# Slab slots, an earlier cache output and a product on GpSimd, in a streaming encoder layer on eight cores

## The reference: what is computed

```
h = rms_norm(x, pre_mix_w); p = h @ w_in      # 1024 x 3584: q k v g | B C hc, 512 columns each
q, k = rotary(q), rotary(k) * 128**-0.5       # 4 heads of 128
o, S = retention in chunks of 64, with decay  # a carried 128 x 128 state per head
o = rms_norm per head(o) * ret_norm_w * silu(g)
y = B * causal_dwconv3(C * hc)
x = x + rms_norm(concat[o, y] @ w_out, post_mix_w)
h2 = rms_norm(x, pre_ffn_w)
u = causal_dwconv3(h2 @ w_up)                 # 1024 x 4096
f = (gelu(u) * (h2 @ w_gate)) @ w_down        # 4096 x 1024
x = x + rms_norm(f, post_ffn_w)
```

## Time and profile before

| what | value |
|---|---|
| median of 3 runs | 2011.95 us (2008.78 to 2012.05) |
| the profiled execution | 2010.04 us |
| its span, core 4, the slowest | 2008.5 us; the other cores 1995.5 to 2005.7 us |
| TensorE busy | 1957.7 us |
| VectorE, ScalarE, GpSimd busy | 1273.2, 970.8, 492.0 us |
| moved by DMA | 369.12 MB, 184 GB/s on average |

### The profile page before, as it was taken

One profiled execution on the slowest core, in us unless ns is written; L12 is line 12 of the kernel. 1 busy time (PEld: TensorE's weight loads), 2 busy tenths in 40 slices (PEclk: granted clock), 3 DMA queues, 4 the chain that ended last, 5 costly groups with the idle time before them and its releaser, 6 DMA issues.

```text
span 2008.5 us, 29808 instructions; the slowest of 8 cores (1995.5 to 2008.5 us)
## 1 busy us (share of the span) xinstructions
PE 1957.7 (97%) x10823; PEld 936.3 (47%) x10823; DVE 1273.2 (63%) x2317; ACT 970.8 (48%) x1922; POOL 492.0 (24%) x1031
## 2 busy tenths in 40 slices
PE   6998999999999999999999999999999999999998
PEld 3453444454444444444444444444444444444443
DVE  6777856667668655674656836668356664567456
ACT  6576685763444453344533445434434445334423
POOL 3653211101422421123221332114121242212001
PEclk9999999999999999999999999999999999999999
DMA  9945888977446634464434643446343553435433
GB/s 283 268 145 163 263 279 273 307 248 258 143 158 204 225 132 157 157 203 147 159 138 178 220 152 116 166 151 230 140 152 130 184 215 126 168 120 190 156 126 117
DMA packets 109955, 369.12 MB, mean 184 GB/s; under 512 B 8952, under 2 KB 43856, under 8 KB 97648
## 3 DMA queue, kind: packets, MB, share of 16 engines
q1 hardware_dynamic: 109536, 367.11, 53.7%
q10 hardware_dynamic: 272, 0.10, 0.0%
HBM read 313.50 MB, written 53.68 MB: 183 GB/s over the span
## 4 chain that ended last, share of the span: by engine, by line
PE 89%; DMA 5%; DVE 2%; ACT 2%; issue 1%; POOL 0%; ACTq 0%; POOLq 0%; SPq 0%; DVEq 0%
PE pF L933 37%; PE pF L1022 20%; PE pM L743 10%; PE pM L782 7%; PE pM L881 5%; DMA x_sb<-xp 2%; PE pM L933 2%; PE pF L743 2%; PE pM L1022 1%; DMA v_sb<-w_down 1%; PE pT L644 1%; PE pT L687 1%; PE pF L782 1%; PE pF L881 1%; DMA kte<-w_gate 1%
## 5 line engine op out<-in xcount | busy, mean ns | idle before, releaser
L933 PE MATMUL pF<-hT,wug 128*128 128x512 bf16 x3856 | 867.2, 380 | 8.8 <-DMA wug<-wug_s 2.1
L933 PEld LDWEIGHTS pF<-hT,wug 128*128 128x128 bf16 x3856 | 373.6, 98 | 448.9 <-issue 5.9
L1022 PE MATMUL pF<-wdn,act 128*128 128x512 bf16 x1846 | 423.9, 380 | 6.0 <-DVE act L944 2.8
L936 ACT ACTIVATE up_sb<-pF 128x512 f32<-128x512 f32 x241 | 143.2, 594 | 344.2 <-PE pF L933 341.6
L939 DVE SCALAR_TENSOR_TENSOR acc<-up_sb,cvec,acc 128x512 f32<-128x512 f32 x256 | 192.4, 752 | 158.7 <-ACT acc L938 158.1
L1022 PEld LDWEIGHTS pF<-wdn,act 128*128 128x128 bf16 x1846 | 179.5, 98 | 219.1 <-DVE act L944 4.1
L944 DVE TENSOR_TENSOR act<-pF,gl 128x512 bf16<-128x512 f32 x230 | 158.4, 689 | 143.3 <-ACT gl L943 127.7
L937 POOL COPY halo_f<-up_sb 128x2 f32<-128x2 f32 x256 | 61.1, 239 | 641.8 <-ACT up_sb L936 641.1
L943 ACT ACTIVATE gl<-acc 128x512 bf16<-128x512 f32 x256 | 160.0, 625 | 118.8 <-DVE acc L941 118.3
L743 PE MATMUL pM<-slab,hT 128*128 128x512 bf16 x856 | 202.6, 383 | 3.8 <-ACT slab L591 2.9
L941 DVE SCALAR_TENSOR_TENSOR acc<-up_sb,cvec,acc 128x512 f32<-128x512 f32 x256 | 198.9, 778 | 5.0
(11 more groups left out here) (380 smaller groups left out, 2242.7 us busy)
## 6 DMA issues: line engine op xcount, KB each, us to landing
wug<-wug_s SPq DMA_DIRECT2D x208, 512.0 KB, 3.8
wdn<-wdn_s SPq DMA_DIRECT2D x28, 2048.0 KB, 8.0
slab<-slab_s SPq DMA_DIRECT2D x54, 1024.0 KB, 5.1
x_sb<-xp SPq DMA_DIRECT2D x32, 512.0 KB, 6.4
stg<-w_up SPq DMA_DIRECT2D x32, 512.0 KB, 9.0
wug_s<-wug SPq DMA_DIRECT2D x32, 512.0 KB, 9.3
yp<-x_sb SPq DMA_DIRECT2D x31, 512.0 KB, 4.2
stg<-w_in SPq DMA_DIRECT2D x18, 512.0 KB, 9.9
```

Of the source, the lines that this page charges most:

```text
L933: op("pe", [lambda e, k=k, u=u, pp=pp: e.matmul(pp[:, :nt], lhsT=wug[:, sl, u, k, :], rhs=hT[:, k, :nt], start=(k == 0), stop=(k == 7)) fo ...
L936: op("act", lambda e: e.activation(out=upv[:, 2:2 + nt], in_=PU[:, :nt], func=AF.Copy), [RU, RUP], [RUP], c_act(nt))
L1022: op("pe", [lambda e, q=q, hs=hs, m=m, cols=cols, pd=pd: e.matmul(pd[:m, :], lhsT=al[q][0][:, cols], rhs=wdn[:, cs_[q] % 8, hs], start=(q ...
```

## The change

It has three parts. In the first mixers there is a fourth slab slot, over wug 2 and 3, and a fixed table says which slab goes where (`SLOT_1`, by slab number: slab 2 to slot 3, 0 to 1, 1 to 2, 3 to 0, 6 to 1, 5 to 3, 4 to 2, 7 to 0, 8 to 1); the staging buffers there are three from the start. The caches of the 16 tokens are put out at the end of the second ffn stage instead of the end of the program. The product with the weight vector at the end of an ffn row group runs on GpSimd, with a planner cost of 2.55 us, except where the row group is ended in halves. `UG_0` and `SL_LEAD` only name values that stood there already.

```diff
+GW_POOL = True
+SLOT_1 = (1, 2, 3, 0, 2, 3, 1, 0, 1)
+UG_0 = 2
+SL_LEAD = 12.0
...
-    STG_M = STG + [(wug[:, q].rearrange("p u k j -> p (u k j)").bitcast(F32), [("wug", q, u, kc) for u in range(2) for kc in range(8)]) for q in range(2, NWUG)]
+    STG_M = STG
...
-    slab_x = wug[:, 0:2].rearrange("p a u k j -> p (a u k j)").rearrange("p (k c) -> p k c", c=512)
-    SLABX = [[("wug", k // 4, (k % 4) // 2, 4 * (k % 2) + q) for q in range(4)] for k in range(8)]
+    slab_x = [wug[:, b:b + 2].rearrange("p a u k j -> p (a u k j)").rearrange("p (k c) -> p k c", c=512) for b in (0, 2)]
+    SLABX = [[[("wug", b + k // 4, (k % 4) // 2, 4 * (k % 2) + q) for q in range(4)] for k in range(8)] for b in (0, 2)]
     def load_slab(first, g):
-        sl = nxt("slab", 3 if first else 2)
-        dst, kk_ = (slab_x, SLABX) if sl == 2 else (SLABS[sl][0], [[k] for k in SLABS[sl][1]])
+        sl = SLOT_1[g] if first else nxt("slab", 2)
+        dst, kk_ = (slab_x[sl - 2], SLABX[sl - 2]) if sl > 1 else (SLABS[sl][0], [[k] for k in SLABS[sl][1]])
-                if g == 8:
-                    ring[0] = STG
-                sa, sr = stage_f32(src, 524288, 30.0 if g == G_FIRST[0] else 12.0)
+                sa, sr = stage_f32(src, 524288, 30.0 if g == G_FIRST[0] else SL_LEAD)
...
         c = 12 * nxt(sk, nm) if sk == "sm" else 6 * nxt(sk, nm)
-        gw = lambda hs: op("dve", lambda e: e.tensor_tensor(out=out_ap[:, hs], in0=src_ap[:, hs], in1=wb_tile[:m, hs], op=ALU.mult),
-                           src_of(hs) + [wb_key], out_of(hs), 0.15 + 0.00106 * (hs.stop - hs.start))
+        gp = GW_POOL and sk == "sf" and part is None
+        gw = lambda hs: op("pool" if gp else "dve", lambda e: e.tensor_tensor(out=out_ap[:, hs], in0=src_ap[:, hs], in1=wb_tile[:m, hs], op=ALU.mult),
+                           src_of(hs) + [wb_key], out_of(hs), 2.55 if gp else 0.15 + 0.00106 * (hs.stop - hs.start))
...
-        sl = (c + 2) % NWUG if first else nxt("wug", NWUG)
+        sl = (c + UG_0) % NWUG if first else nxt("wug", NWUG)
...
+    P.stage = ("F", 1)
+    cache_out(ccs, cfs, z_s, "S", halo_s, "halo_s", "s", 1)
     for t in range(3, 9):
...
     cache_out(ccp, cfp, z, "A", halo_f, "halo_f", "p", 0)
-    cache_out(ccs, cfs, z_s, "S", halo_s, "halo_s", "s", 1)

```

## The result

The change makes the kernel slower: 1.0078 times the time before, 95% interval 1.0061 to 1.0094, that is about 15.7 us on a median of 2011.62 us. The three of its executions that the comparison uses, with disturbed ones left out, took 2025.64, 2027.3 and 2028.31 us. The forecast was 2001.4 us, and its range ended at 2013 us.

The account below looks back on a forecast made before the run. TensorE was taken to bound the kernel. Terms of 3.0 - 5.1 - 4.0 - 4.0 - 0.5 = -10.6 us gave a profiled 1999.4 us, and with 1.9 us for the median 2001.4 us; range 1991 to 2013 us.

Parts of the forecast that it names:

- signs that it had set for being wrong: Products starting before 18 us, the first ffn later than 190 us, or TensorE waiting for VectorE in each later tile.
- What bounds the kernel: Whole span: TensorE, busy 1957.7 of 2008.5 us; only 50.8 us of waits and tail, plus lowered clock, can be won.
- The product on GpSimd: Ffn row group ends: 32 products leave VectorE; in the six later tiles all lies under TensorE, 0 both ways.
- rival C: Six later tiles: GpSimd's product holds up VectorE while chunks start and TensorE waits; 22.6 us, 2024 us; chance 0.12.
- Relief of VectorE at 470 to 510 us: End of the first tile's ffn: shorter TensorE waits for VectorE, 4.0 us gained, bounds 0 and 9.2 us.
- The start: First slab: with three staging buffers, first products 8.0 us late at 24.8 us; net loss 3.0 us, bounds 0 and 8.0.
- The end of the first mixers and the first ffn: First out_proj and first ffn's start: the new slots let loads and casts run earlier, gaining 5.1 and 4.0 us.
- second term: First ffn's start: earlier casts of chunks 2 and 3 gain 4.0 us; bounds 0 (norms' chain sets pace) and 10.6.
- first term: End of the first mixers: w_out slabs load in time, shorter wait and full clock gain 5.1 us; bounds 3.0 and 6.8.
- Rival B: The ffn's two gains don't come, as ScalarE's norms and loads of x set the pace; 2009.3 us; chance 0.18.
- The caches: The 16 tokens' caches, moved from tail to second ffn stage's end: 0, up to 1 us.
- The tail: Kernel's end: third row group's product no longer ahead of VectorE's last addition, 0.5 us less; bounds 1.2 less, 1 more.

Follow-up runs that it names:

- e2: The kernel before with only the product with the weight vector moved to GpSimd; it costs 0.64%.
- e8: The kernel before with only the product on GpSimd, each but a tile's first waiting for the x update of the row group before; ratio 0.9995.
- e1: The change with the product back on VectorE, so slab slots and early caches only, against the kernel before; ratio 1.0007.
- e9: The change's slots and caches, product on VectorE, five staging buffers until the sixth slab, casts of chunks 0 to 3 after the last convolution work; ratio 1.0003 to before.
- e4: The kernel before with the product on GpSimd only in the first two ffn stages; hardly anything gained, the ratio's interval reaches down to 0.9989.
- e15: The whole change, with each GpSimd product but a tile's first waiting for the x update of the row group before; ratio 1.0024 to the kernel before.

## Why the prediction was wrong, point by point

The forecast was 10.6 us less, and 15.7 us more was measured. Two of the signs that it had set for being wrong came: TensorE waits for VectorE about once in each later tile, and the first ffn starts later than 190 us, at 191.5 to 201.4 us on the eight cores (183.7 to 190.3 us before).

**What bounds the kernel** was read rightly: TensorE's work is the same, and all that changed was its waits, their clock and the tail.

**The product on GpSimd: the step that failed.** The forecast was 0 for the six later tiles. It measured 8.9 us from 634 us to the tail alone (e2) and 12.6 us in the change. The failed step is the argument against rival C: that most products run "while TensorE works on w_down, without such additions". I looked for operations with two inputs in SBUF among the convolution's additions alone. The update of x reads the sums and x, both in SBUF, stands right beside the products, and is among the rows that I had read (L660 in the earlier trace rows). Counted over the eight cores of the profile after, 144 of the 216 updates from `f_acc` overlap a product and take 2.46 us on average, the other 72 take 1.28 us; 24 of the convolution's first taps overlap one, with a mean of 2.06 instead of 0.75 us. The additions to the ffn sums, which read one input from PSUM, take 0.684 us whether they overlap a product (216) or not (1328). The Trainium skill's rule that I had cited (page "SBUF — State Buffer", section "SBUF: two separate sides": two SBUF inputs on VectorE against a GpSimd operation that reads SBUF, for the whole instruction) fits these three counts. I gave the rival that it speaks for 0.12, and weighed an observation of 0.94 us for one operation against a whole queue.

The price was mis-sized as well. Rival C took 0.94 us for each of 24 products, 22.6 us. In fact an update that overlaps a product costs about 1.2 us more on average, and one that is held 1.9 us (3.17 us instead of 1.28), but TensorE feels only what is left once for each tile: six waits of together 9.7 us for a chunk, where the same core had one of 1.3 us before, and 4.6 us in two waits for a norm. So C's 2024 us, close to the profiled 2027.3 us, is right in mechanism and place but near in number by luck: its 22.6 us is too much, and it kept 10.6 us of gains that mostly did not come.

**Relief of VectorE at 470 to 510 us: right mechanism, two thirds of the size.** Forecast 4.0 us. e2 gains 2.7 us from 211 to 475 us, and 3.2 by 634 us; there too updates are held. With products behind the updates the gain is 4.0 us by 475 us (e8, 0.9 + 3.1), as forecast.

**The start: a mis-sized term.** Forecast 3.0 us with bounds of 0 and 8.0 us; the change is 6.1 us late at 54 us, within the bounds, and 12.4 us at 146 us. The first product starts at 27.45 us and not at 24.8. The step that failed is the sentence that three buffers feed a slab in 10.5 us, "so I expect no starving". I counted bytes at the full rate. But a buffer is not refilled before its casts are done, and a cast whose piece is late holds the evacuations behind it; ScalarE waited 18.2 us for such pieces on core 1. How much of the 12.4 us each of these makes is not measured.

**The end of the first mixers and the first ffn: the places right, the gain conditional.** Forecast 5.1 and 4.0 us, 9.1 together. The wait of 5.05 us for the last slab's cast is gone, the casts of chunks 2 and 3 run by 173 us, and the change makes up 7.0 us between 146 and 211 us, e1 8.3 us. But e9, with the same slots at the end, gives nothing to a TensorE that is on time. The lower bound of the second term, 0 if the norms' own chain sets the pace, is the nearest to what happened, and it would have had to stand for the first term too. That the chain is what takes the gain is argued, as said above. Rival B kept the first term and named ScalarE's norms and the loads of x; e9's waits are for VectorE.

**The caches: right**, 0, ratio 1.0000.

**The tail: wrong sign.** Forecast 0.5 us less, measured 2.2 us more from TensorE's last matmuls to the end. VectorE of the kernel after:

```profile
2010.54 3.05 DVE L663 SCALAR_TENSOR_TENSOR x_sb<-f_acc,stat_f,x_sb 128x1024 f32<-128x1024 f32 x1
...
2016.62 2.11 DVE L661 TENSOR_TENSOR f_acc<-f_acc,wb_post_ffn 128x512 f32<-128x512 f32 x1
```

Here even the last row group's own product, of 512 columns and 0.68 us, took 2.11 us, beside GpSimd's product of the group before it. That bound (1 more) was too narrow, for the same reason as above.

## What to carry to other kernels

Before moving an elementwise operation to GpSimd, list every VectorE instruction that can run beside it and reads two operands from SBUF, and price each at its own length plus what is left of the GpSimd instruction; the additions here that read one operand from PSUM were not held. If the move still pays, order the two (a dependency on the neighbour) and limit it to the stage in which TensorE waits for VectorE; that was worth 0.3 to 0.4% here, the free form cost 0.6%. And in a queue that is worked in order a late load delays all that stands behind its cast: price fewer staging buffers by that work and not by their bytes alone. A gain at a later place can be nothing but an earlier delay made good: e1 gained 8.3 us where e9, on time, gained none.

## What the runs showed of the hardware

- The hold works in both directions and appears as duration, not as a wait. GpSimd's root had a mean of 1410 ns beside VectorE's product; with that product gone it is 767 ns (L672 of the kernel after), and 551 ns in the mixers.
- An operation with a single tensor input was held too: the scaling of x to bf16 (L644, 0.745 us) took up to 2.749 us beside a product (core 1). The same section of the Trainium skill counts VectorE's two-port performance modes among what the lock concerns; no run here separates the mode from the operation.
- In the profiles of e1 to e4 TensorE was granted a level of 0.81 in stretches, mostly 15.03 us long on cores 0 to 3 and 2.4 to 9.0 us on cores 4 to 7; in no other profile here. Windows of e1 on core 3, one in such a stretch and one between two of them, both without a gap in TensorE's work:

```profile
897.60:912.50 14.90, 14.90 (x65) 6.44 (x64) 10.95 (x18) 8.85 (x16) 4.01 (x9) 0.81 0.98 302
1154.80:1377.70 222.90, 222.90 (x1158) 106.15 (x1157) 132.76 (x231) 94.17 (x186) 52.30 (x106) 1.00 0.44 152
```

The kernel before was 1% slower beside these four (2031.98 against 2011.62 us), more than any edit here moved it; only ratios of runs made side by side could be compared. The record gives e1 to e4 and e9 to e15 the same chip number, so whether the level belongs to a chip or to the hour is not shown.
